# The rows of x behind the norms of the first block: from VectorE to GpSimd

## The reference, cut to what matters

```python
def layer_norm(x, g, b):
    xf = x.astype(jnp.float32)
    mu = jnp.mean(xf, axis=-1, keepdims=True)
    var = jnp.mean(jnp.square(xf - mu), axis=-1, keepdims=True)
    y = (xf - mu) * lax.rsqrt(var + LN_EPS) * g.astype(jnp.float32) + b.astype(jnp.float32)
    return y.astype(x.dtype)

def first_block(x, mem, ...):
    for l in range(DEPTH):
        x = layer_norm(DN_ALPHA * x + 0.5 * swiglu_ffn(x, ffn_w_in[l, 0], ffn_w_out[l, 0]), ln_g[l, 0], ln_b[l, 0])
        x = layer_norm(DN_ALPHA * x + mixer_sublayer(x, ...), ln_g[l, 1], ln_b[l, 1])
        x = layer_norm(DN_ALPHA * x + memory_cross_attention(x, mem, ...), ln_g[l, 2], ln_b[l, 2])
        x = layer_norm(DN_ALPHA * x + 0.5 * swiglu_ffn(x, ffn_w_in[l, 1], ffn_w_out[l, 1]), ln_g[l, 3], ln_b[l, 3])
    return x
```

## Time and profile before

| what | value |
|---|---|
| median of three runs | 2697.38 us (2695.96 to 2697.62) |
| the profiled execution | 2689.54 us |
| its span, first to last instruction | 2687.7 us |
| TensorE matmuls busy | 2563.5 us, 95% |
| VectorE busy | 1695.4 us, 63%, 2507 instructions |
| ScalarE busy | 1257.5 us, 47% |
| GpSimd busy | 174.7 us, 6%, 215 instructions |
| mean granted TensorE clock | 0.983 |

### The profile page before, as it was taken

How to read it: one execution, slowest core, us unless ns; L and a number is a source line. 1 busy time by engine, 2 the same in 40 slices (tenths; PEclk the granted TensorE clock), 3 DMA queues, 4 the chain that set the end, 5 groups by cost and what they waited for, 6 DMA issues and landing times. The chain is left out here.

```text
span 2687.7 us, 48607 instructions
## 1 busy us (share of the span) xinstructions
PE 2563.5 (95%) x16525; PEld 2211.2 (82%) x16525; DVE 1695.4 (63%) x2507; ACT 1257.5 (47%) x1798; POOL 174.7 (6%) x215
## 2 busy tenths in 40 slices
PE   8999999999999999999999998899999999898999
PEld 8998877888889888877888886687898887666898
DVE  5556776765566465867665767776556555765655
ACT  4435445544344345444454554455444443553443
POOL 1000000010020000000010201200000011100000
PEclk9999999999999999999999999999999999999999
DMA  7655455566576564555555534553456668435554
GB/s 240 211 180 163 142 177 187 168 219 240 191 222 220 185 217 123 168 155 198 189 187 180 153 109 158 177 157 101 162 174 213 229 206 212 156 95 164 186 184 141
DMA packets 276177, 479.67 MB, mean 178 GB/s; under 512 B 17616, under 2 KB 87320, under 8 KB 275872
## 3 DMA queue, kind: packets, MB, share of 16 engines
q1 hardware_dynamic: 265632, 445.24, 51.9%
q0 software_dynamic: 10304, 31.31, 3.9%
HBM read 475.33 MB, written 6.92 MB: 179 GB/s over the span
## 5 line engine op out<-in xcount | busy, mean ns | idle before, releaser
L122 DVE TENSOR_TENSOR wlo<-raw,whi 128x1024 fp32r<-128x1024 f32 (+3 forms) x786 | 911.3, 1172 | 728.0 <-ACT whi L163 604.0
L163 ACT ACTIVATE whi<-raw 128x1024 fp32r<-128x1024 f32 (+3 forms) x786 | 785.4, 1015 | 626.7 <-PE bank L171 422.1
L171 PE MATMUL bank<-xh,whi 128*128 128x256 f32 x2208 | 632.3, 286 | 13.9 <-DVE xk L128 7.1
L171 PE MATMUL bank<-xl,whi 128*128 128x256 f32 x2208 | 624.8, 283 | 0.0
L171 PE MATMUL bank<-xh,wlo 128*128 128x256 f32 x2208 | 624.6, 283 | 0.0
L171 PEld LDWEIGHTS bank<-xh,whi 128*128 128x128 f32 x2208 | 421.9, 191 | 29.6 <-issue 17.8
L171 PEld LDWEIGHTS bank<-xl,whi 128*128 128x128 f32 x2208 | 422.0, 191 | 1.1 <-issue 0.5
L171 PEld LDWEIGHTS bank<-xh,wlo 128*128 128x128 f32 x2208 | 421.8, 191 | 0.0
L171 PE MATMUL bank<-whi,xh 128*128 128x512 f32 (+2 forms) x632 | 257.9, 408 | 21.1 <-issue 7.7
L171 PE MATMUL bank<-whi,xl 128*128 128x512 f32 (+2 forms) x632 | 249.7, 395 | 0.0
L171 PE MATMUL bank<-wlo,xh 128*128 128x512 f32 (+2 forms) x632 | 248.5, 393 | 0.0
(11 more groups left out here) (432 smaller groups left out, 3870.5 us busy)
## 6 DMA issues: line engine op xcount, KB each, us to landing
raw<-in_ffn_w_in SPq DMA_DIRECT2D x280, 512.0 KB, 4.6
raw<-in_ffn_w_out SPq DMA_DIRECT2D x154, 512.0 KB, 4.6
raw<-in_w_mix_in SPq DMA_DIRECT2D x112, 512.0 KB, 3.6
raw<-in_mod_w SPq DMA_DIRECT2D x96, 512.0 KB, 4.9
raw<-in_od_w_in SPq DMA_DIRECT2D x40, 512.0 KB, 4.6
raw<-in_ffn_w_in SPq DMA_DIRECT2D x56, 256.0 KB, 3.0
raw<-in_w_branch SPq DMA_DIRECT2D x24, 512.0 KB, 3.6
raw<-in_ev_w_in SPq DMA_DIRECT2D x24, 512.0 KB, 3.9
```

Source lines behind the costliest of these rows:

```text
L122: return Made(self.e and self.e.tensor_tensor(out, a, b, op))
L163: return Made(self.e and self.e.activation(out, a, f, **k))
L171: return Made(self.e and self.e.matmul(out, lhs, rhs, **k))
```

## The change

In `rows`, the multiplication by lg and the addition of lb are issued by GpSimd (`co.po`) in place of VectorE (`co.dv`), and they count up GpSimd's semaphore. Nothing else is edited: tiles, order of the code and readers of x are the same.

```diff
             for t in range(2):
                 x = co.x[:, t, :]
-                co.dv.wait_ge(co.lnpar, co.xfree, n[t])
-                a = co.dv.tensor_tensor(x, y[:, t, :], co.lg[:, :], ALU.mult).then_inc(co.s_dv)
+                co.po.wait_ge(co.lnpar, co.xfree, n[t])
+                a = co.po.tensor_tensor(x, y[:, t, :], co.lg[:, :], ALU.mult).then_inc(co.s_po)
                 yield
-                co.dv.wait_ge(a)
-                out.append(co.dv.tensor_tensor(x, x, co.lb[:, :], ALU.add).then_inc(co.s_dv))
+                co.po.wait_ge(a)
+                out.append(co.po.tensor_tensor(x, x, co.lb[:, :], ALU.add).then_inc(co.s_po))
                 if t == 0:
                     yield
```

## The result

| kernel | median (lowest to highest) | runs | the profiled execution, its span | mean granted clock |
|---|---|---|---|---|
| before | 2696.67 us (2693.72 to 2697.62) | 4 | 2689.54, 2687.7 us | 0.983 |
| after | 2710.93 us (2707.44 to 2712.71) | 4 | 2707.44, 2705.2 us | 0.979 |

The ratio of after to before is 1.0060, 95% interval 1.0047 to 1.0073: the change makes the kernel slower by 14.3 us of medians (16 us by the ratio). The forecast was 2714.0 us and slower.

What follows compares the result with a forecast made beforehand. TensorE, matmuls filling 95% of the span, bounds the kernel. 14.4 + 1.7 + 0.5 = 16.6 us on the profiled 2689.54 us gives 2706.1 us, plus 7.84 us to the median 2714.0 us; whole range 2695 to 2725 us.

Steps and rivals of the forecast that it cites:

- places 1 and 2: Mixer to cross attention, layers 0 and 1, where TensorE waits for xk: each resumes 7.2 us later.
- Length of one: One x operation of 128x1024 on GpSimd, taken as twice VectorE's 1.22 us: 2.44 us.
- GpSimd is first, y waits: Place 1: GpSimd's first x operation starts 0.11 us before y, which waits 2.33 us.
- Two wlo held: Place 1: second and third x operations go ahead of the first and second wlo, 2.44 us each.
- The term of 14.4 us: The delay of TensorE's restart at places 1 and 2 together, 7.2 us at each.
- The clock: Place 1: TensorE's longer stop brings one stretch at 0.50 clock, half of 3.4 us, adding 1.7 us.
- The last place: Around x<-x,lb at 1355.4 us, before TensorE's wait for cy: between -1.1 and +1.5 us, taken as +0.5 us.
- Nothing at the four other places: Remaining sublayer boundaries: wlo held up to 2.4 us several times against a margin of 6 us, costing zero.
- Rival 1: VectorE is not held by GpSimd; only 1.1 us gained at the last place, 2696 us; chance 0.22.
- Rival 2: VectorE held only once at each place, 2 x 2.4 us, no clock change: 2702 us; chance 0.12.
- Rival 3: GpSimd's operation takes 4 us and more, about 29 us in all: 2726 us and up; chance 0.09.
- Rival 4: Something on TensorE's path counted as hidden shortens, such as xsm and xl: faster by over 5 us; chance 0.03.

Runs made afterwards that it cites:

- The halves: Changed kernel with each GpSimd x operation issued as two of 128x512: 2702.01 us, ratio 1.0030 to the kernel before.
- the other order: Changed kernel, but at places 1 and 2 GpSimd takes the second half of x first: 2705.39 us, ratio 1.0038 to the kernel before.
- the kernel with places 1 and 2 alone: Against the kernel before, only the 8 x operations at places 1 and 2 moved to GpSimd: 2708.51 us, ratio 1.0057.
- the kernel that leaves places 1 and 2 alone: Against the kernel before, 20 x operations moved to GpSimd, those at places 1 and 2 kept on VectorE: 2696.80 us, ratio 1.0004.

## Why the prediction was right

It held in its mechanism at places 1 and 2, where the cost lies, and in its sum by errors that cancel.

- *Length of one.* Taken 2.44 us from twice VectorE's row; measured 2.34 for the product and 2.38 for the addition at the shortest. No row bounded the factor of two from above, so that it came out close is in part luck. By the Trainium skill, "GPSIMD Engine Reference", section "Performance versus the Vector engine", the estimate was 2.25 us; the trace lies between the two.
- *GpSimd is first, y waits.* Forecast 2.33 us, measured 2.75 - 0.81 = 1.94. The wait was counted in full, but y, with 0.81 us of its own, ends only 0.54 us after GpSimd's product: some 0.27 us of its length overlap with the hold. The rows that the forecast read as evidence had a wlo beside GpSimd and no y; that y, which reads one tile, is held too was taken without a row and came true.
- *Two wlo held.* Forecast 2.44 us each, measured 6.73 - 2.35 = 4.38 together, 2.19 each, with the same kind of overlap. The instructions that read PSUM are not held, as assumed. Place 1: 6.3 us instead of 7.2; place 2 the same. The term of 14.4 us is 12.6 us. The halves, the other order and the kernel with places 1 and 2 alone show that the term is right in kind: 3.3, 3.3 and 6.25 us for each place.
- *The clock.* Forecast 1.7 us at place 1 and nothing at place 2. The trace has 10.2 us of half clock at either; by the ledger they cost 10.1 - 8.0 = 2.1 us and 13.7 - 13.2 = 0.5 us. That longer stops bring such a stretch was right, the size too low.
- *TensorE's stops.* Forecast was one stop of about 10 us ahead of xh,whi at either place. It is split: 2.37, 2.20 and 4.15 us at place 1, 2.37 and 8.63 us at place 2, since the late y stops TensorE as well. The delay in all is what was forecast, less the overlaps.
- *The last place.* Forecast +0.5 us between -1.1 and +1.5; measured 15.3 - 13.9 = +1.4 us, the upper end. The runs showed that no single value is right: with the order of two instructions 0.14 us apart the other way, the kernel that leaves places 1 and 2 alone has about zero there.
- *Nothing at the four other places.* Right. Single wlo are held there up to 4.26 us, as the tile wlo of the changed kernel shows between 200 and 260 us:

```profile
L122 DVE TENSOR_TENSOR wlo<-raw,whi x18: 1211/1225/4259, 202.2 to 258.0; 128x1024 fp32r<-128x1024 f32 x18
```

Yet the ledger has no step behind the x operations there, and the kernel with 20 operations on GpSimd is at most 0.15% slower than before by the upper end of its interval. A wlo that takes 3 us more is inside the margin of 6 us.
- *The sum.* 12.6 + 2.6 + 1.4 = 16.6 us, the forecast's number with other parts: the holds were put 1.8 us too high, clock and last place together 1.8 us too low, and that these agree is luck. Medians differ by 14.3 us. The forecast put the sum onto the first median, 7.84 us above its own profiled execution, and that execution was one of the fastest. The granted clock goes with a part of this spread: in the 23 runs of before the three with a clock of 0.983 average 2689.5 us, the other twenty between 2692.3 and 2697.4 us by their clock.

*The rivals.* Rival 1 (VectorE not held) is excluded by the y of 2.75 us. Rival 2 (held once for each place) is wrong for this kernel, three holds stand there; that its kind exists is shown by the second half first, where y and the first wlo pass and one full hold and half a one remain. Its argument from the power on 128x3 did carry over in one spot: the x operation at 781.96 us was passed by two wlo in a row and took 3.83 us. At places 1 and 2 the engines took turns instead. The rows of before had shown both, and why the one or the other happens stays open. Rival 3 (4 us and more) is excluded by the 2.34 and 2.38 us, though single instructions reach 3.8 us with their waiting. Rival 4 (a hidden gain on TensorE's path) is not seen: moving x away from VectorE alone, at five boundaries, gives a ratio of 1.0004.

## What to carry to other kernels

Work moved from VectorE to GpSimd can still be paid for by VectorE. Here it was, almost wherever VectorE's next instruction read two tiles of SBUF, or was y, while GpSimd worked on x; and nearly the whole price came from the two places where VectorE's chain had no room. In no kernel tried here did work taken off VectorE this way make it faster. So look at the chain beside which the moved work will run, and not at VectorE's share of busy time; if it must be moved, keep it off that chain (1.1 us left of 14.3, not clear of zero), or make GpSimd wait until the chain has passed (4.1 us left), or keep its instructions short (7.9 us left). The same rows showed the better lever: the two wlo ahead of xk that nobody needed yet, put behind it at each place, took 4.9 us off TensorE's stops, of which 4.1 us were kept.

## What was not expected of the hardware

- A copy of 128x1024 on GpSimd takes 1.03 us and a fill 0.95 us, but a product or sum of two tiles 2.34 to 2.38 us. With copies the pair of wlo was held 1.7 us, with products and additions 4.4 us: the price of sharing hangs on the length of GpSimd's instruction.
- Holding works in both directions. At the last place a lead of 0.14 us went with either a wlo of 1.23 us beside a GpSimd operation of 3.37 us, or 3.33 us beside 2.38 us. Elsewhere a wlo 0.45 us ahead was held, and one 0.35 us behind was not, so the starts in the trace do not foretell it everywhere.
- A held VectorE instruction is shown as busy: the busy time rose by 17.5 us with 28 instructions fewer. Held time is found in the lengths of single instructions and not in the idle times.
